# A two-layer diffusion trunk on one core: another order of loads and multiplications at the start of the first layer

## The reference, cut to what matters

```python
mc = _modulation(c_ctx[None], w_mod[l], b_mod[l])      # silu(c) @ w_mod + b_mod, split into 6 parts
ml = _modulation(c, w_mod[l], b_mod[l])
h = _rmsnorm(xc, norm_mix[l]) * (1.0 + mc[1]) + mc[0]  # the latent tokens likewise with ml
aq, ak, av, bq, bk, bv, cq, ck, cv, cg, gates = _split_projection(h, w_in[l])
```

## Time and profile before

| | |
|---|---|
| Median of 3 runs | 2033.26 us (2031.02 to 2035.55) |
| The profiled execution | 2033.99 us, with a span of 2032.2 us |
| PE busy | 1860.2 us (92%) |
| DVE, ACT, POOL busy | 607.8, 342.1 and 35.6 us |
| Moved by DMA | 552.36 MB, at 272 GB/s over the span |

### The profile page before, as it was taken

The page is one execution under the profiler, slowest core; times in us unless marked ns, Lnnn a source line. Parts: engine busy times, 40 slices in busy tenths (PEclk is TensorE's granted clock), DMA queues, the critical chain, the costliest instruction groups (busy, mean ns, idle before and its releaser), DMA issues.

```text
span 2032.2 us, 19307 instructions
## 1 busy us (share of the span) xinstructions
PE 1860.2 (92%) x8062; PEld 929.0 (46%) x8062; DVE 607.8 (30%) x1178; ACT 342.1 (17%) x787; POOL 35.6 (2%) x22
## 2 busy tenths in 40 slices
PE   6999999999999988788789999999998998887886
PEld 2565556555544333233255555565554343333322
DVE  2332346454311101101042323755534102010103
ACT  4032331000211001000141323210003010100002
POOL 0100000000000000000020000000000000000000
PEclk8999999999999999999989999999999999999998
DMA  9322281442589999999972221616325999999995
GB/s 390 149 94 88 84 328 56 166 166 103 207 347 429 429 428 428 430 429 428 427 287 93 84 88 66 276 42 248 124 97 234 398 429 429 428 429 429 429 428 228
DMA packets 53254, 552.36 MB, mean 272 GB/s; under 512 B 5808, under 2 KB 10800, under 8 KB 12208
## 3 DMA queue, kind: packets, MB, share of 16 engines
q1 hardware_dynamic: 49392, 548.51, 65.0%
q10 hardware_dynamic: 3776, 2.62, 0.4%
HBM read 546.91 MB, written 4.19 MB: 271 GB/s over the span
## 4 chain that ended last, share of the span: by engine, by line
PE 64%; DMA 30%; DVE 3%; ACT 1%; issue 1%; SPq 0%; DVEq 0%; ACTq 0%
PE psum L871 12%; PE psum L1040 12%; PE psum L738 12%; DMA ring<-in_w_down 8%; PE psum L955 6%; PE psum L740 6%; DMA ring<-in_w_up 6%; PE psum L968 4%; DMA dense<-in_w_up 4%; DMA dense<-in_w_gate 4%; DMA ring<-in_w_gate 4%; DMA wide<-in_w_gate 3%; PE psum L395 2%; DMA ring<-in_w_mod 2%; PE psum L1020 1%; PE psum L790 1%
## 5 line engine op out<-in xcount | busy, mean ns | idle before, releaser
L738 PE MATMUL psum<-hT,ring 128*128 128x384 f32 x768 | 260.9, 494 | 8.4 <-ACT hT L1170 8.2
L871 PE MATMUL psum<-hT,ring 128*128 128x384 f32 x768 | 255.7, 486 | 0.0
L1040 PE MATMUL psum<-dense 128*64 128x512 f32 x864 | 195.4, 596 | 30.5 <-DMA dense<-in_w_up 17.5
L1040 PE MATMUL psum<-ring,dense 128*64 128x512 f32 x832 | 188.2, 596 | 28.4 <-DMA ring<-in_w_gate 14.6
L738 PEld LDWEIGHTS psum<-hT,ring 128*128 128x128 f32 x768 | 145.6, 193 | 104.4 <-issue 13.7
L871 PEld LDWEIGHTS psum<-hT,ring 128*128 128x128 f32 x768 | 145.6, 190 | 100.9
L1702 DVE TENSOR_TENSOR state<-state,psum 128x512 f32<-128x512 f32 x32 | 22.0, 687 | 376.1 <-PE psum L1040 338.0
L1040 PEld LDWEIGHTS psum<-dense 128*64 128x64 f32 x864 | 62.5, 137 | 153.3 <-issue 128.9
L955 PE MATMUL psum<-dense,ring 128*128 128x384 f32 x384 | 131.9, 487 | 0.0
L1040 PE MATMUL psum<-ring,square 128*64 128x512 f32 x512 | 115.2, 595 | 17.9 <-DMA ring<-in_w_down 17.9
L740 PE MATMUL psum<-ring,hT 128*128 128x512 f32 x288 | 126.5, 592 | 0.0
(11 more groups left out here) (200 smaller groups left out, 1615.5 us busy)
## 6 DMA issues: line engine op xcount, KB each, us to landing
ring<-in_w_up SPq DMA_DIRECT2D x32, 2048.0 KB, 38.3
ring<-in_w_down SPq DMA_DIRECT2D x32, 2048.0 KB, 40.1
ring<-in_w_in SPq DMA_DIRECT2D x60, 1024.0 KB, 11.1
dense<-in_w_up SPq DMA_DIRECT2D x30, 2048.0 KB, 40.0
dense<-in_w_gate SPq DMA_DIRECT2D x24, 2048.0 KB, 35.5
wide<-in_w_down SPq DMA_DIRECT2D x20, 2048.0 KB, 40.2
ring<-in_w_gate SPq DMA_DIRECT2D x20, 2048.0 KB, 36.7
wide<-in_w_gate SPq DMA_DIRECT2D x20, 2048.0 KB, 38.1
```

The source lines that it names most:

```text
L738: last = M.matmul(psum[:, bank, 0:T], ring[:, n % RING, k, cols], hT[:, k, :], start=k == 0, stop=k == KD - 1)
L871: last = M.matmul(psum[:, Z[1], 0:T], ring[:, n_gate % RING, k, (j % 4) * P:(j % 4 + 1) * P], hT[:, k, :], start=k == 0, stop=k == KD - 1)
L1040: last = M.matmul(psum[HALF * half:HALF * (half + 1), bank, :], lhsT(k), w[:, kk, half * SLAB:(half + 1) * SLAB], start=k == 0, stop=k == ...
```

## The change

In layer 0 SP loads `x` ahead of the modulation slabs, which now come in the order 0, 2, 1, 3. The layer's vectors come after the second of them. The first half of the first `w_in` slab is issued between modulation slabs 1 and 3, the second half behind slab 3. PE multiplies the first half of `w_in` (chunks 0 to 3 of groups 0 and 1) ahead of modulation slab 3, and that of group 2 between the product and the transposes of slab 3. The sums stay in their PSUM banks until the groups are completed; group 2 gets bank `O[0]`. The modulation steps of layer 0 use the banks `S` in place of `Z`. `mod1_ready` counts two steps in both layers: shift and scale of chunks 0 to 3, then of 4 to 7. In layer 0 ACT modulates chunks 0 to 3 after the first step, ahead of its reads of slabs 1 and 3, and the rest after the second.

```diff
-        START_MODS = [[0, 1, 2, 3], [2, 3]]
+        START_MODS = [[0, 2, 1, 3], [2, 3]]
...
-        START_FILL = [[("mod", 0, 0), ("mod", 0, 1), ("modT", 0, 0), ("mod", 0, 2), ("modT", 0, 1), ("mod", 0, 3), ("modT", 0, 2), ("modT", 0, 3)],
+        START_FILL = [[("mod", 0, 0), ("modT", 0, 0), ("mod", 0, 2), ("modT", 0, 2), ("mod", 0, 1), ("modT", 0, 1), ("mod", 0, 3), ("modT", 0, 3)],
...
-            return (S if FILL[f] in START_FILL[1] else Z)[f % 2]
+            if FILL[f] == ("z", 0, 2):
+                return O[0]
+            return (S if FILL[f] in START_FILL[0] + START_FILL[1] else Z)[f % 2]
...
+                sp.dma_start(xT[:], x_in).then_inc(x_loaded, 16)
                 load_slab(0, 0)
-                sp.dma_start(xT[:], x_in).then_inc(x_loaded, 16)
-                for n in range(1, len(START_MODS[0])):
-                    load_slab(0, n)
+                load_slab(0, 1)
                 sp.dma_start(vecT_all[:], layer_vectors).then_inc(vec_in, 16)
+                load_slab(0, 2)
+                wait_slab_free(sp, 0, 0)
+                load_half(0, RING, 0)
+                load_slab(0, 3)
+                load_half(0, RING, 1)
...
+                    def z_first_half(g):
+
+                        n = SLABS[0].index(("w_in", 0))
+                        if g == 0:
+                            first_half_here(n)
+                        for k in range(KD // 2):
+                            if g == 0:
+                                chunk_ready_wait(pe, 0, 0, k)
+                            M.matmul(psum[:, filler_bank(f_of("z", 0, g)), 0:T], ring[:, n % RING, k, g * P:(g + 1) * P], hT[:, k, :],
+                                     start=k == 0, stop=False)
...
-                        for k in range(KD):
+                        begun = l == 0 and g < 3
+                        for k in range(KD // 2 if begun else 0, KD):
...
-                        fill(START_FILL[0][:3])
+                        fill(START_FILL[0][0:1])
                         norm_sum(TR[0], KD)
-                        fill(START_FILL[0][3:])
+                        fill(START_FILL[0][1:6])
+                        z_first_half(0)
+                        z_first_half(1)
+                        fill(START_FILL[0][6:7])
+                        z_first_half(2)
+                        fill(START_FILL[0][7:8])
...
-                        read(START_FILL[0][:3])
+                        read(START_FILL[0][0:1])
                         inverse_rms(TR[0], 1)
-                        read(START_FILL[0][3:])
+                        read(START_FILL[0][1:4])
+                        sc.wait_ge(mod1_ready, 1)
+                        modulate(0, scale_mix, 0, 0, KD // 2)
+                        read(START_FILL[0][4:])
...
-                    sc.wait_ge(mod1_ready, at(mod1_ready, 1))
-                    modulate(0, scale_mix, 0)
+                    sc.wait_ge(mod1_ready, at(mod1_ready, 2))
+                    modulate(0, scale_mix, 0, KD // 2 if layer == 0 else 0)
...
-                        finish_mods(layer, 0, 3)
-                        finish_scale(layer, scale_mix_all, slice(8, 16), slice(48, 56)).then_inc(mod1_ready, 1)
-                        dve.wait_ge(mod1_ready, at(mod1_ready, 1))
+                        for part in range(2):
+                            finish_mods(layer, part, part)
+                            finish_mods(layer, 2 + part, 2 + part)
+                            finish_scale(layer, scale_mix_all, slice(8 + 4 * part, 12 + 4 * part), slice(48 + 4 * part, 52 + 4 * part),
+                                         slice(4 * part, 4 * part + 4)).then_inc(mod1_ready, 1)
+                        dve.wait_ge(mod1_ready, at(mod1_ready, 2))
```

More of the change, by code:

```diff
@@ L300, in build @@
         rs_ready = sem("rs_ready", 2)
-        mod1_ready = sem("mod1_ready", 1)
+        mod1_ready = sem("mod1_ready", 2)
         mod2_ready = sem("mod2_ready", 1)
@@ L558, in _, with load_half, load_slab @@
             def _(sp):
-                def load_slab(layer, n):
+                def load_half(layer, n, part):
                     to, of = slab_into(layer, n), slab_source(layer, n)
                     half = to.shape[1] // 2
-                    sp.dma_start(to[:, 0:half], of[:, 0:half]).then_inc(slab_in[n % RING], 16)
-                    sp.dma_start(to[:, half:], of[:, half:]).then_inc(slab_rest[n % RING], 16)
+                    rows = slice(half * part, half * (part + 1))
+                    sp.dma_start(to[:, rows], of[:, rows]).then_inc((slab_in, slab_rest)[part][n % RING], 16)
+                def load_slab(layer, n):
+                    load_half(layer, n, 0)
+                    load_half(layer, n, 1)
                 sp.dma_start(silu_c[:], cvec).then_inc(rows_in, 16)
                 sp.dma_start(const[:, 0:CONST_HEAD], const_in[:, 0:CONST_HEAD]).then_inc(head_in, 16)
+                sp.dma_start(xT[:], x_in).then_inc(x_loaded, 16)
                 load_slab(0, 0)
-                sp.dma_start(xT[:], x_in).then_inc(x_loaded, 16)
-                for n in range(1, len(START_MODS[0])):
-                    load_slab(0, n)
+                load_slab(0, 1)
                 sp.dma_start(vecT_all[:], layer_vectors).then_inc(vec_in, 16)
+                load_slab(0, 2)
[3 more added lines that the diff above has]
+                load_half(0, RING, 1)
                 for layer in range(DEPTH):
@@ L599, in _ @@
                     early_at = [SLABS[layer].index(x) for x in (("w_in", 13), ("branch", 2), ("w_in", 14))]
-                    for n in range(first_w_in if layer == 0 else 0, len(SLABS[layer])):
+                    for n in range(first_w_in + 1 if layer == 0 else 0, len(SLABS[layer])):
                         if n == (first_w_in + 1 if layer == 0 else RING):
@@ L1163, in inverse_rms, with modulate @@
                         A_.activation(rs[:], rs[:], ACT.Exp, scale=-0.5).then_inc(rs_ready, 1)
-                    def modulate(mixer, scale, shift):
-                        for k in range(KD):
+                    def modulate(mixer, scale, shift, first=0, last=KD):
+                        for k in range(first, last):
                             if k not in DVE_MODULATES[mixer]:
@@ L1198, in read_z @@
                             s = SCALE if chunk in (CK, CK + 1) else 1.0
-                            A_.activation(zT[:, chunk, :], psum[:, Z[f % 2], 0:T], ACT.Copy, scale=s).then_inc(z_read, 1)
+                            A_.activation(zT[:, chunk, :], psum[:, filler_bank(f), 0:T], ACT.Copy, scale=s).then_inc(z_read, 1)
                     def read_norm(l, t):
@@ L1427, in finish_mods, with finish_scale @@
                                          vecT_all[:, l, cols].unsqueeze(2).to_broadcast([P, n, 2]), ALU.add))
-                def finish_scale(l, out, rows, gain):
-                    return V.scalar_tensor_tensor(out=out[:, l], in0=modT_all[:, l, rows, :], scalar=1.0,
-                                                  in1=vecT_all[:, l, gain].unsqueeze(2).to_broadcast([P, KD, 2]), op0=ALU.add, op1=ALU.mult)
+                def finish_scale(l, out, rows, gain, chunks=slice(0, KD)):
+                    n = chunks.stop - chunks.start
+                    return V.scalar_tensor_tensor(out=out[:, l, chunks], in0=modT_all[:, l, rows, :], scalar=1.0,
+                                                  in1=vecT_all[:, l, gain].unsqueeze(2).to_broadcast([P, n, 2]), op0=ALU.add, op1=ALU.mult)
                 dve.wait_ge(head_in, 16)
```

## The result

| | before | after |
|---|---|---|
| Median of 18 runs | 2033.37 us (2030.79 to 2035.63) | 2037.72 us (2035.10 to 2040.20) |
| Ratio to before | | 1.0020, 95% interval 1.0014 to 1.0026 |
| Profiled execution, its span | 2033.99, 2032.2 us | 2036.85, 2035.0 us |

The change costs 4.35 us by the medians and 2.86 by the two profiled executions. The forecast was +2.7 and 2036.0, with a range of 2031.5 to 2040.5. The chance given to slower by over 0.2% was 0.32; the measured ratio lies on that bound.

A forecast was written before the change was run, and what follows sets the result against it. Start of layer 0 bound by slab loads, then ACT's modulation and decay work, then PE, with shifts passed on in full: +2.1 at group 2's end plus 0.6 in layer 1 gives +2.7, median 2036.0 us, range 2031.5 to 2040.5.

The forecast's parts named there:

- Slab 3 multiplied at 34, not at its landing: Layer 0, PE: slab 3 lands at 31.1 but is multiplied from 34.3, behind the first halves of groups 0 and 1.
- second mod1_ready near 41: Layer 0: shift and scale of chunks 4 to 7 ready at 40.6 against 32.8 before, 7.8 later.
- The added wait on ACT: Layer 0: slab 1's read queues behind modulating chunks 0 to 3 (3.57), so w_in's first half begins at 29.0, not 26.1.
- PE would idle 4 us for ACT's read of group 0: Layer 0, before group 2: PE ready 6.4 behind the second mod1_ready, ACT's read only lets it start at 10.6.
- the 6.99 of the working: Layer 0: time from ACT's first decay factor (39.36) to PE's group 2 (46.35), taken as unchanged.
- Group 2's half, a gain of 2.7: Layer 0, PE: group 2 needs only half a group once started, a gain of 2.7.
- The three terms: Layer 0, to group 2's end: +7.8 mod1_ready, -2.95 from there to PE's start, -2.7 group 2's half; +2.1 in all.
- The clock rival: Layer 0: PE idles before slab 1's transposes, w_in halves run at half rate; +4.2 to +7, 2037.5 to 2040.3, chance 0.29.
- Layer 1: Start of layer 1: DVE's small steps become six, not three, on the chain before ACT's modulation; +0.6.
- PE not held by ACT: Layer 0: group 2 begins when PE gets there, ending at 49.7; -2.1, with layer 1 -1.5, 2031.8; chance 0.07.
- Swallowed later: After layer 0's start: the shift disappears in a wait PE has anyway; 2033.3 to 2034, chance 0.10.
- the yardstick: End of group 2 in layer 0: 51.78 before, forecast 53.9, so +2.1.

The follow-up runs named there:

- a_warm: Changed kernel plus five unread products on PE between groups 1 and 2 of layer 0: 2036.06 us, ratio 1.0012 to before.
- a_layer1: Changed kernel with layer 1's first modulation finished in three DVE steps, not ten: 2038.66 us, ratio 1.0020 to before.
- a_order: Changed kernel with PE in layer 0 taking slab 3's product and transposes right behind group 0's first half: 2032.34 us, ratio 0.9991 to before.
- a_both: Changed kernel with ACT's early reads of groups 0 and 1 and slab 3 behind group 0's first half, ten DVE steps kept: 2031.69 us, ratio 0.9987.
- a_read: Changed kernel with ACT in layer 0 reading group 0 ahead of the in_decay activations and group 1 behind them: 2032.27 us, ratio 0.9994 to before.
- a_all: Changed kernel with ACT's early reads, slab 3 behind group 0's first half, and layer 1's three DVE steps: 2028.20 us, ratio 0.9977 to before.
- a_warm2: Changed kernel with unread PE products: four between slab 1's product and transposes, five between groups 1 and 2: 2036.64 us, ratio 1.0015 to before.

## Why the prediction was right, and where it was off

- **Slab 3 multiplied at 34, not at its landing; second mod1_ready near 41.** It began at 34.52, and ACT's modulation of chunk 4 at 40.65, for 34.3 and 40.6 in the working. Of the steps between, the first mod1_ready was 24.6 for 24.0 and the first half began at 29.26 for 29.0. That the times agree so closely is in part luck. The working starts from a landing at 13.5, and in this execution it was 14.34. From the landing to the second mod1_ready the working has 27.1, and the trace 26.31: its steps were 0.8 too long in all, and the late landing covered it.
- **The added wait on ACT.** As forecast, the read of slab 1 stood behind the eight activations (3.61 for 3.57), and the transposes and the halves of w_in behind that.
- **PE would idle 4 us for ACT's read of group 0.** It idled 3.43; the read began at 50.23 and PE at 50.77, 10.12 behind mod1_ready for 10.6. The difference lies ahead of ACT's first decay factor (43.78, so 3.13 for 3.6); the rest took the 6.99 of the working.
- **Group 2's half, a gain of 2.7: mis-sized.** The prediction saw that a low clock in the second halves hides in the idle time. It did not ask what this idle time does to the clock afterwards. The half took 4.54, and from PE's start to the rotation 4.38 for 5.26: 0.9 were gained, not 2.7. The three terms as measured are +7.84 (mod1_ready, 40.65 for 32.81), -3.42 (from there to PE's start 10.12 for 13.54) and -0.88, so +3.54 where +2.1 was forecast. With the 0.87 of the landing taken out the first is +6.97 for 7.8 and the sum +2.67: the error of 1.8 on one side is in good part made up by 0.8 and 0.5 on the other, which is luck. That the last term is the clock's is shown by a_warm beside a_layer1.
- **The clock rival** had its place in the first halves. It happened there in four of the eight profiles that keep the changed kernel's loads (a_order 4.44 and a_both 3.98 for 2.75, a_warm 6.41 and a_layer1 6.39 for 5.33). In the other four (after, a_read, a_all, a_warm2) it fell earlier, under slab 1's product (3.3 to 3.5 for 1.92), where ACT's modulation hides it but for a_warm2. Ahead of slab 1's product PE had been idle for 1.84 to 1.88 in these four and for 0.86 to 1.56 in the others. Its price can be read from after and a_layer1, whose programs in layer 0 are the same: distances of 40.81 and 42.89, so 2.1, inside the 1.6 to 2.7 of the working. I gave it 0.29; by these profiles it is nearer to a half. That it makes the upper group of after's runs is likely (a_layer1's profiled run has 2038.96) but not shown; after was profiled in the other case only. The rule of the Trainium skill named with it (TensorE: Matmul & The Clock Gate, Part 1: idle time takes the clock back) agrees with the 0.50 at 51.9 to 54.9.
- **Layer 1.** The number of steps was miscounted: ten and not six. Each `finish_mods` is two instructions and there are four of them, which I had counted rightly in layer 0. The cost on DVE is 1.2; that the +0.6 lies near the 0.5 seen at the end of group 2 (0.8 over the twelve profiles) is luck.
- **PE not held by ACT** was a rival with -1.5. a_read makes it true by another order of ACT, and gave a ratio of 0.9994 against before, -1.2 us, with an interval that reaches +0.6. **Swallowed later** is refuted: 3.54 at 55 us is 3.51 at 505, and over the twelve profiles a later end of group 2 comes out at the end of the span in full.
- **A reading of the earlier trace rows.** The working says that DMA's tenths stand at 9 only in the experts. The first slice has a 9 too; it is the start that the change is about, and the working itself counts with its 426 GB/s.

The forecast of 2036.0 fell short of the median by 1.7. The profiles give 2.67 at the yardstick and 0.5 to 0.8 in layer 1, 3.2 to 3.5 for 2.7 forecast; the medians give 4.35. What is left, about 1, is as large as the differences that the clock makes between runs, and its cause isn't shown.

## What to carry to other kernels

Before work is moved ahead of a late input, ask what ends last behind that input. Here the bound behind it was the tail of another engine, and PE was given shorter work only to idle; the same move paid once ACT's reads and PE's order were changed too (a_all, a ratio of 0.9977); with ACT's reads alone it came out even (a_read, 0.9994). Work put in front of an input that has landed delays it by its whole length (slab 3's product began at 34.52 behind two first halves and at 31.87 behind one in a_all): begin only what fits into the wait.
A forecast idle stretch of PE needs a second question, which is at what clock PE comes out of it.

## What the runs showed of the hardware

An idle stretch of 3.43 us that followed full-rate matmuls was followed by a clock of 0.50: in after the clock was still at 1.00 when PE resumed at 50.77 and low from 51.9 at the latest, in a_layer1 it was low as PE resumed (0.55 from 52.26 to 52.80). Either way the price falls on the work behind the gap, here 1.7 us on a piece of 2.8 (4.54 for 2.85). In another execution the clock fell with a gap of only 2.1 us in front (a_warm2, groups 0 and 1 in 7.26 for 5.57), and the same 2.12 cost nothing in a_read. The runs of one kernel lie up to 5 us apart (2035.1 to 2040.2); how much of that is the clock's isn't shown. A single profile can mislead by some of it: after's own is 0.9 below its median.
